# Shifting the slots of a weight ring by 64 bytes each in SBUF

## The reference

```
for layer in range(2):
    y = rmsnorm(h, g0)
    y = even_mixer(y) if layer == 0 else odd_mixer(y)   # w_in, attention, w_out
    h = h + rmsnorm(y, g1)
    u = rmsnorm(h, g2) @ w_up                           # 1024 x 5632
    c = causal depthwise convolution of width 3 over u
    gate, val = split(c)
    h = h + rmsnorm((gelu(gate) * val) @ w_down, g3)    # 2816 x 1024
```

## The kernel before, in words

| tensor | start modulo 512 |
|---|---|
| h, xn, xpair, raw, whi, wlo, vbuf, qkT, hid_hi, hid_lo, conv, act_g, hidf | 128 |
| xb_parts, sb_sp, sb_sphi, sb_splo, probs | 32 |
| c_mask | 352 |
| c_identb, wg_parts | 96 |
| c_gpre | 480 |

## Time and profile before

### The profile page before, as it was taken

One profiled execution on the slowest core, in us unless ns is written; L12 is line 12 of the kernel. 1 busy time (PEld: TensorE's weight loads), 2 busy tenths in 40 slices (PEclk: granted clock), 3 DMA queues, 4 the chain that ended last, 5 costly groups with the idle time before them and its releaser, 6 DMA issues.

```text
span 655.8 us, 9975 instructions
## 1 busy us (share of the span) xinstructions
PE 646.6 (99%) x3572; PEld 539.4 (82%) x3574; DVE 460.1 (70%) x627; ACT 385.1 (59%) x561; POOL 163.8 (25%) x123
## 2 busy tenths in 40 slices
PE   9999999999999999999999999999999999999996
PEld 6888887577888888888888888777888888888885
DVE  6498766877697878786457645676688788886532
ACT  7556355865757667666335535765567676767330
POOL 0323300001053444441001000680123434343000
PEclk9999999999999999999999999999999999999999
DMA  8987633004456363637652663304255554544601
GB/s 350 339 296 284 228 129 129 1 6 189 132 198 245 133 249 131 236 149 268 242 196 69 253 240 144 129 1 192 97 184 200 182 202 168 216 151 177 248 1 64
DMA packets 18971, 115.60 MB, mean 176 GB/s; under 512 B 2911, under 2 KB 3453, under 8 KB 6013
## 3 DMA queue, kind: packets, MB, share of 16 engines
q1 hardware_dynamic: 17789, 111.52, 45.7%
q10 hardware_dynamic: 1152, 3.67, 1.7%
HBM read 114.14 MB, written 1.05 MB: 176 GB/s over the span
## 4 chain that ended last, share of the span: by engine, by line
PE 93%; DVE 2%; POOL 2%; ACT 1%; issue 1%; DVEq 0%; POOLq 0%
PE ps L1423 27%; PE ps L1430 14%; PE ps L1380 11%; PE ps L1381 11%; PE ps L1382 11%; PE ps L1452 5%; PE ps L1507 2%; POOL sb_splo L1352 1%; PE ps L1751 1%; PE ps L1635 1%; PE ps L1371 1%; PE ps L1901 1%; PE ps L1679 1%; PE ps L1601 1%; PE ps L1738 1%
## 5 line engine op out<-in xcount | busy, mean ns | idle before, releaser
L778 DVE TENSOR_TENSOR wlo<-raw,whi 128x2048 fp32r<-128x2048 f32 x99 | 227.0, 2325 | 72.7 <-ACT whi L413 72.6
L413 ACT CAST whi<-raw 128x2048 fp32r<-128x2048 f32 x99 | 185.7, 1916 | 48.6 <-PE ps L1382 42.0
L1423 PE MATMUL ps<-xpair,whi 128*128 128x512 f32 x768 | 183.4, 391 | 0.0
L1423 PEld LDWEIGHTS ps<-xpair,whi 128*128 128x128 f32 x768 | 141.2, 188 | 27.6
L1430 PEld LDWEIGHTS ps<-xpair,wlo 128*128 128x128 f32 x768 | 98.5, 191 | 3.7
L1430 PE MATMUL ps<-xpair,wlo 128*128 128x256 f32 x768 | 99.6, 283 | 0.0
L1328 POOL TENSOR_TENSOR hidf<-act_g,conv 128x512 f32<-128x512 f32 x22 | 76.1, 3460 | 85.0 <-ACT act_g L671 85.0
L1380 PE MATMUL ps<-whi,hid_hi 128*128 128x512 f32 x176 | 68.5, 389 | 0.0
L1381 PE MATMUL ps<-wlo,hid_hi 128*128 128x512 f32 x176 | 68.5, 389 | 0.0
L1382 PE MATMUL ps<-whi,hid_lo 128*128 128x512 f32 x176 | 68.5, 389 | 0.0
L1380 PE MATMUL ps<-whi,xpair 128*128 128x512 f32 x168 | 67.7, 403 | 0.0
(11 more groups left out here) (197 smaller groups left out, 788.2 us busy)
## 6 DMA issues: line engine op xcount, KB each, us to landing
raw<-in_weights SPq DMA_DIRECT2D x101, 1024.0 KB, 5.0
c_gpost<-in_gpost ACTq DMA_DIRECT2D x4, 512.0 KB, 5.0
raw<-in_weights SPq DMA_DIRECT2D x3, 512.0 KB, 6.8
c_gpre<-in_gpre ACTq DMA_DIRECT2D x3, 512.0 KB, 4.3
h<-in_x SPq DMA_DIRECT2D x2, 512.0 KB, 3.8
out<-h SPq DMA_DIRECT2D x4, 256.0 KB, 2.0
raw<-in_weights SPq DMA_DIRECT2D x2, 256.0 KB, 4.8
t<-in_masks SPq DMA_DIRECT2D x1, 512.0 KB, 12.1
```

The lines of the kernel that those rows point to most:

```text
L413: act.copy(whi[:, slot, :], raw[:, slot, :]).then_inc(hi_done, 1)
L778: dve.tensor_tensor(wlo[:, slot, :], raw[:, slot, :], whi[:, slot, :].bitcast(F32), ALU.subtract).then_inc(lo_done, 1)
L1423: pe.matmul(ps[:, b0 + m, :], whi[:, slot, cols], xpair[:, kt].rearrange("p a c -> p (a c)"), start=kt == 0, stop=kt == KT - 1, skip_group ...
```

## The change

Each slot of `whi` and `wlo` gets 16 float32 (64 bytes a partition) behind it that nothing reads or writes. The slots of `whi` move by 0, 64, 128 and 192 bytes. `wlo` begins 256 bytes later and its slots move by 256, 320, 384 and 448. What lies behind `wlo` moves by 512 bytes. `raw` stays. There is room: the last tensors end at 209,536 bytes, where the right side begins at 209,664.

```
+GAP = 16
...
-        whi = sb("whi", [P, RING, UNIT], F32R)
-        wlo = sb("wlo", [P, RING, UNIT], F32R)
+        whi = sb("whi", [P, RING, UNIT + GAP], F32R)[:, :, 0:UNIT]
+        wlo = sb("wlo", [P, RING, UNIT + GAP], F32R)[:, :, 0:UNIT]
```

## The result

The changed kernel takes 661.68 us (median of 4 runs, 661.60 to 661.83) against 657.68 for the kernel before beside it: a ratio of 1.0063, 95% interval 1.0051 to 1.0075. It is slower by 0.6%, outside the predicted range of 656.2 to 658.9. The profiled span is 659.8 us, 4.0 more than before.

A forecast was written before the change was run, and what follows sets the result against it. TensorE, 93% of the span, was taken to bound the kernel through its matmul spacing. Matmuls and splits were each priced at 0, so the 655.8 us span stayed and the forecast was 657.5 us, range 656.2 to 658.9.

The forecast's parts named there:

- the ceiling of 31.4 us: Largest possible gain: 2364 matmuls meeting a moved slot, times the 13.3 ns each has on top of streaming.
- that part of the sum, 0: Splits and casts reading the weight buffers: no address conflict visible to be cured, so 0 us.
- so I take 0 for both: Pricing of weight matmuls: moved slots change nothing, 0 us, whether the slot is the moving or the stationary operand.
- The first row, L1605: bf16 matmul, operands 256 bytes apart: starts 0.23 us apart like the weight matmuls, taken as evidence for zero.
- place 0: The common start modulo 512 bytes that activations and all weight slots had before the change.
- The second, L1751: Slots moving against a 64-column stationary operand 96 bytes away: 117 ns against L1430's 119.4, taken as evidence for zero.
- The third, L1901 with L1903: Pair of 384 and 128 columns, operands at 32 and 96: 0.28 us, so other places cost at most some 4 ns.
- sum by parts: Expected time of the L1901 and L1903 pair: 109 ns plus 160 + 13.3, giving 282 ns against 286 seen.
- The rival that came true by its size: Slower, chance 0.05: moving operands off place 0 cost 4 ns in 1020 matmuls, 4.1 us, giving 661.6 us.
- The other rival: Faster, chance 0.07: weight load and moving operand meet at place 0; ending that saves 26 us, giving 631.5 us.
- L1380 to L1382 above 231 ns with L1423 unchanged: Sign of being wrong on the slow side: matmuls with moving slots slow down, those with stationary slots do not.
- The pattern of period four: Sign of being wrong on the fast side: spacings towards 215 ns in moved slots, 227 kept for whi slot 0.

The follow-up runs named there:

- e8: Against the kernel before: no gaps, all slots of whi and wlo start 256 bytes past the activations; 657.52 us, ratio 0.9999.
- e4: Against the kernel before: no gaps, whi slots stay, all wlo slots start 64 bytes past the activations; 660.82 us, ratio 1.0049.
- e7: Against the kernel before: weight slots keep their places modulo 512, the activations xpair move by 64 bytes instead; 658.18 us, ratio 1.0010.
- e13: The kernel before, places unchanged, with 64 stationary columns loaded instead of 128 in 672 of 768 L1423 matmuls; 661.4 us, one run.

## Why the prediction was wrong

**The bound, and the sizes.** TensorE's stream bounds the kernel, and the time of the change could only come from the spacing of its matmuls: this held, to the last 0.1 us. The 2760 matmuls are right, and the ceiling of 31.4 us was never near (by e8 it counts too many: slot 0 of wlo moved by 256 bytes, which is no move). No other engine, wait or transfer entered the sum, as said. The splits kept their durations (2287 and 1912 ns), so that part of the sum, 0, was right.

**The step that failed** is "so I take 0 for both", and under it the reading of three rows.

- The first row, L1605, was taken as a matmul away from place 0 with an unchanged spacing: "c_mask, whose place is 256 bytes from that of its stationary c_identb". But 256 bytes are difference 0, as e8 shows. The row was the old case over again. I had looked at distances modulo 512, because the change was described that way, without asking whether a smaller period would hide the effect.
- The second, L1751, has a difference of 160 with another width of load, so that no row of before tells what it would have taken at 0. I named that flaw and used the row nevertheless, as the nearest.
- The third, L1901 with L1903, has 96 - 32 = 64. It was the one row that could have shown the effect, and I put it down as a bound. Its sum by parts was wrong too: from the 384 columns to the 128 it is 442.46 - 442.24 = 0.22 us, and from there to the next 0.06 (224 and 60 ns in the finer times), not 173 and 109. That 286 came out near 282 was chance, and whether the 4 ns are this effect is not shown: no run moved these operands against each other.

```profile
442.46 0.22 PE L1903 MATMUL ps<-sb_splo,wg_parts 128*128 128x128 f32 x1
```

What the runs showed in place of that 0: the spacing of the weight matmuls follows the difference of the two starts modulo 256 bytes, here plus 3.89 us for moving slots, plus 2.07 for L1423 and minus 1.80 for L1430.

**The rival that came true by its size.** "A moving operand off place 0 costs 4 ns" gave 661.6 us, and 661.68 was measured. Its own term, 4.1 us, is near the measured 3.89, but by luck: the three slots that it counts do not cost 4 ns each but about 2, 6 and 6.6 (229, 233 and 233 ns in the down projection), and the low weights of slot 0, which it counts as well, cost nothing. Its other half, that a stationary slot off place 0 costs nothing, was wrong twice over: L1423 lost 2.07 us and L1430 gained 1.80, which cancel. "4 ns more would be hidden: a load fits in 109 ns, and its cover is 120 or 227" does not hold: L1423 rose to 233.7 ns in slot 1 under that very cover, and the row of L1903 has a matmul with a load of its own only 60 ns before the next. The total hides this; the chain by slot shows it at once. I gave this rival 0.05, and nothing in the rows supported so little: of the three rows that were to speak for zero, the first repeats the old difference, and the second, the one named against it, compares two widths of load.

**The other rival.** A gain of 26 us from a meeting of two reads at one place: no layout came near 215 ns. The largest gain at any place was 6.7 ns, on the 256-column matmuls.

**Signs named ahead.** "L1380 to L1382 above 231 ns with L1423 unchanged" was half seen: 230.8 and 231.1 ns on average, but L1423 changed too. The pattern of period four was seen, with slot 0 at the old pace in the down projection.

**The two pages.** The Trainium skill (SBUF — State Buffer, "Who interferes with whom") has TensorE read through two independent ports and wait on no one; by that rule none of the layouts would differ from 657.6 us. The runs decide against using it so: up to 666.6 us from places alone. Whether it is the ports that disagree, these runs do not show. The rule of the other page (TensorE: Matmul & The Clock Gate, "Wait — 56ns, not 53.3ns?"), 216 ns for 512 columns, was met by no weight matmul at any place.

**What stays open.** Shown: the spacing depends on the difference of the starts modulo 256, on neighbouring matmuls (e4) and on what ran before (e7, two rhythms at the same places). Not shown: what inside TensorE or SBUF makes it so. The obvious account, that the next load's reads meet the moving stream, expected less from half a load and e13 showed more. Differences that are not multiples of 32 bytes were not tried.

## What to carry to other kernels

Give the operands of long rows of 512-column matmuls starts that are equal modulo 256 bytes, all of them, and check it when tensors in front of them change size: here 32 bytes of padding in front of both weight rings cost 1.3%. For matmuls of 256 columns equal starts were the slowest in the table above. Read the start-to-start distance by ring slot, not its mean, since gains and losses of single slots cancel in the mean. And when a row is to show that an address does not matter, compute its distance for every period that the effect could have, not for the one that the change names.

## What the runs showed of the hardware that was not expected

- At a granted clock of 1.00 the start-to-start distance of F32R matmuls of 512 columns goes from 226.7 to 233.3 ns with the starts of the two operands in SBUF, and that of 256 columns from 120 down to 113.3. The period is 256 bytes, and the sign counts: 233 ns at 64, 229 at 192.
- It settles into rhythms that repeat to within a nanosecond or two: 227, 227, 226 at difference 0; 231, 236 at 64; 226, 229, 232 at 192. At 192 bytes the 256-column matmuls have two, 113.3 and 117.7 ns, in units that alternate.
- Weight loads of 64 columns in place of 128 came with slower 512-column matmuls, 230 ns in place of 227 (e13, one run).
